# A two-block kernel on one core: reordered entries into three stages, work moved to GpSimd, and the residual ahead of the modulation's products

## The reference, cut to what matters

```python
h_lat = h_lat + m_lat[2] * o_lat                      # layer 0: RWKV and Mamba mixer
h_lat = h_lat + m_lat[5] * _swiglu(_modulate(_rms_norm(h_lat, g), m_lat[3], m_lat[4]), w1, w3, w2)
# and the same for h_ctx
def prepare(h):                                       # in the mixer
    z = h @ w_in
    z_rw = _centred_shift(z[..., :RW_COLS], rw_mu[0], rw_mu[1])
    ...
    bonus_f = jnp.sum(rh * k_dir[:, :, 0] * rw_r_k[0], axis=-1, keepdims=True)
    bonus_b = jnp.sum(rh * k_dir[:, :, 1] * rw_r_k[1], axis=-1, keepdims=True)
    bonus = (bonus_f + bonus_b) * vh
    xbc = jax.nn.silu(_centred_dwconv(xbc, mb_conv_w, mb_conv_b))
    dt = jax.nn.softplus(dt_raw + mb_dt_bias)
    a_neg = -jnp.exp(mb_a_log)
m_lat = jnp.split(c_lat_act @ w_ada[i] + b_ada[i], 6) # the modulation, of every layer
out = sum(gates[..., e] * _swiglu(h, w1[e], w3[e], w2[e]) for e in range(8))  # layer 1: top 2 of 8 experts
```

## Time and profile before

| | us |
|---|---|
| runs | 3094.3, 3093.96, 3085.2 |
| median | 3093.96 |
| profiled execution, its own time | 3092.86 |
| its span, first to last instruction | 3091.1 |
| PE busy | 2966.1 |
| DVE busy | 1315.6 |
| ACT busy | 539.9 |
| mean granted TensorE clock | 0.980 of full speed |

### The profile page before, as it was taken

How to read it: one execution, slowest core, us unless ns; L and a number is a source line. 1 busy time by engine, 2 the same in 40 slices (tenths; PEclk the granted TensorE clock), 3 DMA queues, 4 the chain that set the end, 5 groups by cost and what they waited for, 6 DMA issues and landing times.

```text
span 3091.1 us, 50586 instructions
## 1 busy us (share of the span) xinstructions
PE 2966.1 (96%) x21484; PEld 1949.7 (63%) x21484; DVE 1315.6 (43%) x3023; ACT 539.9 (17%) x1200; POOL 0.2 (0%) x4
## 2 busy tenths in 40 slices
PE   7999899999999998999999999999999899999998
PEld 5455699994444443557745555445558678877887
DVE  1467788875998977403321111111111432023211
ACT  2113433321211111203310000000011310022000
POOL 0000000000000000000000000000000000000000
PEclk9999899999999999999989999999999999999999
DMA  7232001004776885320189999999972235522451
GB/s 267 94 136 81 1 1 42 1 15 136 231 238 226 250 239 164 136 95 15 51 329 378 373 370 375 378 392 387 373 272 91 79 105 154 145 87 68 150 150 55
DMA packets 351331, 551.01 MB, mean 178 GB/s; under 512 B 14256, under 2 KB 292144, under 8 KB 347792
## 3 DMA queue, kind: packets, MB, share of 16 engines
q1 hardware_dynamic: 351120, 547.89, 50.3%
HBM read 546.80 MB, written 1.05 MB: 177 GB/s over the span
## 4 chain that ended last, share of the span: by engine, by line
PE 90%; DVE 5%; ACT 2%; DMA 2%; issue 1%; SPq 0%; DVEq 0%; ACTq 0%
PE bank L675 16%; PE bank L1342 15%; PE bank L1134 9%; PE bank L1358 7%; PE bank L1535 7%; PE bank L936 7%; PE bank L1148 4%; PE bank L634 3%; PE bank L754 3%; PE bank L1175 2%; PE bank L1079 2%; DVE mix L2093 2%; PE bank L920 1%; DMA arena<-in_ada_w 1%; PE bank L1209 1%; PE bank L1301 1%
## 5 line engine op out<-in xcount | busy, mean ns | idle before, releaser
L675 PE MATMUL bank<-a,ring 128*128 128x256 f32 (+1 forms) x1792 | 451.2, 414 | 8.9 <-DVE a L2028 6.6
L2093 DVE SCALAR_TENSOR_TENSOR mix<-arena,csil,mix 128x256 f32<-128x256 f32 x1008 | 402.1, 477 | 45.9 <-ACT mix L1638 45.9
L675 PEld LDWEIGHTS bank<-a,ring 128*128 128x128 f32 x1792 | 340.6, 191 | 116.2 <-issue 64.2
L1342 PE MATMUL bank<-ring,arena 128*32 128x352 f32 x5376 | 404.8, 461 | 4.8 <-DVE small L2652 4.8
L1342 PEld LDWEIGHTS bank<-ring,arena 128*32 128x32 f32 x5376 | 176.8, 110 | 227.8 <-issue 226.8
L1134 PE MATMUL bank<-a,ring 128*128 128x512 f32 x704 | 307.6, 597 | 6.8 <-ACT a L1634 6.8
L1134 PEld LDWEIGHTS bank<-a,ring 128*128 128x128 f32 x704 | 133.2, 191 | 179.9 <-issue 177.9
L1535 PE MATMUL bank<-arena,ring 128*128 128x256 f32 x1024 | 223.5, 379 | 2.0 <-DVE arena L2805 2.0
L2688 DVE TENSOR_TENSOR arena<-arena,bank 128x352 f32<-128x352 f32 x48 | 25.0, 521 | 443.4 <-ACT arena L1902 443.4
L1358 PE MATMUL bank<-ring,arena 128*32 128x256 f32 x3840 | 213.3, 379 | 0.0
L1535 PEld LDWEIGHTS bank<-arena,ring 128*128 128x128 f32 x1024 | 194.4, 190 | 29.1 <-DVE arena L2805 2.8
(11 more groups left out here) (416 smaller groups left out, 3195.7 us busy)
## 6 DMA issues: line engine op xcount, KB each, us to landing
ring<-in_moe_w SPq DMA_DIRECT2D x224, 704.0 KB, 9.2
ring<-in_moe_w SPq DMA_DIRECT2D x160, 512.0 KB, 6.7
ring<-in_mlp_w SPq DMA_DIRECT2D x64, 1024.0 KB, 5.4
arena<-in_ada_w SPq DMA_DIRECT2D x96, 512.0 KB, 3.8
arena<-in_w_ada SPq DMA_DIRECT2D x48, 512.0 KB, 3.5
ring<-in_ffn_w SPq DMA_DIRECT2D x22, 1024.0 KB, 8.3
arena<-in_moe_w SPq DMA_DIRECT2D x32, 704.0 KB, 10.0
h<-in_w_ada SPq DMA_DIRECT2D x8, 2048.0 KB, 7.4
```

Source lines behind the costliest of these rows:

```text
L675: i = mm(bank[b][:, 0:n], ws[:, k, t * P:t * P + P], rhs[:, k, sl], start=(k == 0), stop=(k == KT - 1))
L1342: i = mm(b[32 * t:32 * t + 32, 0:PART], ac_[:, g, 32 * k:32 * k + 32], by_tile(ws[i_], t), start=(k == 0), stop=(k == KT - 1), skip_group_ ...
L2093: ins = V.scalar_tensor_tensor(dst, x, cond, dst, ALU.mult, ALU.add)
```

## The change

Six edits; the computation stays as it is.

1. Mamba's entry. PE does half of `rkv_tile(0)`, turns chunks 0 and 1 as soon as the SiLU tiles that each needs are there, then `gram`, a quarter of `rkv_tile(0)`, chunks 2 and 3, the last quarter, `cs`, `decay(0)` and `rkv_tile(1)` without the wait for `shift(0)`. ACT does the softplus after the second `xbc` copy, DVE's part comes ahead of convolution 5.
2. `keys_by_query` of j = 0 and 1, as four operations each, and the clearing of `state` go to GpSimd.
3. In the second product the residual and its square stand ahead of the modulation's products and first parts of that step.
4. At the experts' entry the turning of the gathered tokens and the two marks come ahead of the overflow order.
5. The output leaves in four DMAs of 256 KB.

The sixth is only the place of `cs` and `shift(0)` on DVE, behind `xdt`. The diff, cut:

```diff
@@ sync
-            sy.wait_ge(act_done, at(AC, ("norm", 12, KT - 1, 1)))
-            sy.dma_start(out.rearrange("(k p) n -> p k n", p=P), hT[:, :, LAT]).then_inc(stored, 16)
-            sy.wait_ge(stored, 16)
+            for k in range(0, KT, 2):
+                sy.wait_ge(act_done, at(AC, ("norm", 12, k + 1, 1)))
+                sy.dma_start(out.rearrange("(k p) n -> p k n", p=P)[:, k:k + 2, :], hT[:, k:k + 2, LAT]
+                             ).then_inc(stored, 16)
+            sy.wait_ge(stored, 4 * 16)
@@ tensor
-            rkv_tile(0)
+            rkv_tile(0, range(0, 4))
+            pe.wait_ge(act_done, at(AC, ("zg", 3)))
+            pe.wait_ge(act_done, at(AC, ("xb", 3)))
+            turned_x(0)
+            turned_x(1)
+            pe.wait_ge(act_done, at(AC, ("xb", 5)))
+            turned_b(0)
+            turned_b(1)
             pe.wait_ge(act_done, at(AC, ("xb", 7)))
...
             i.then_inc(pe_done, did(PE, "gram"))
+            rkv_tile(0, range(4, 6))
+            pe.wait_ge(vec_done, at(VE, ("bt", 0)))
+            turned_x(2)
+            turned_b(2)
+            pe.wait_ge(vec_done, at(VE, ("bt", 1)))
+            turned_x(3)
+            turned_b(3)
+            rkv_tile(0, range(6, KT))
...
+                    if u == 0:
+                        rkv_tile(1)
                     pe.wait_ge(vec_done, at(VE, ("shift", u)))
-                    rkv_tile(u + 1)
+                    if u:
+                        rkv_tile(u + 1)
...
-                pe.wait_ge(vec_done, at(VE, ("rk", j)))
+                if j < 2:
+                    pe.wait_ge(pool_done, at(GP, ("rk", j)))
+                else:
+                    pe.wait_ge(vec_done, at(VE, ("rk", j)))
@@ scalar
+            for j in range(2):
+                xbc_copy(j)
             ac.wait_ge(vec_done, at(VE, "dt_raw"))
...
             act(a_neg, row("mb_a_log", 16), ACT.Exp).then_inc(act_done, did(AC, "a_neg"))
+            for j in range(2, 8):
+                xbc_copy(j)
+            for j in range(8):
+                ac.wait_ge(vec_done, at(VE, ("conv", j)))
+                act(xb[:, j, :], xb[:, j, :], ACT.Silu).then_inc(act_done, did(AC, ("xb", j)))
...
             for k in range(KT):
-                if k + 1 < KT:
-                    first_parts(pairs_of(FT + k + 2))
                 later_rows_out(FT + k)
                 ac.wait_ge(vec_done, at(VE, ("ffn res", k)))
                 square(2, slice(0, T), k)
+                if k + 1 < KT:
+                    first_parts(pairs_of(FT + k + 2))
...
+            counts.count[ACM] = per
+            act(small[:, 700:701], ident[:, 0:1], ACT.Copy).then_inc(ac_moe, per)
             ac.wait_ge(vec_done, at(VE, "blocks"))
-            counts.count[ACM] = per
-            act(small[:, 700:701], small[:, 604:605], ACT.Copy).then_inc(ac_moe, per)
@@ gpsimd (new)
+            for j, spare in ((0, 1), (1, 3)):
+                gp.wait_ge(vec_done, at(VE, ("kd", 1, j)))
+                G.tensor_scalar(kdka[:, j, :], kd[0][:, j, :], col("rw_r_k", j), None, ALU.mult
+                                ).then_inc(pool_done, did(GP, ("rk 0", j)))
+                G.tensor_scalar(kdka[:, spare, :], kd[1][:, j, :], col("rw_r_k", 4 + j), None, ALU.mult
+                                ).then_inc(pool_done, did(GP, ("rk 1", j)))
+                gp.wait_ge(pool_done, at(GP, ("rk 1", j)))
+                G.tensor_tensor(kdka[:, j, :], kdka[:, j, :], kdka[:, spare, :], ALU.add
+                                ).then_inc(pool_done, did(GP, ("rk 2", j)))
+                gp.wait_ge(pool_done, at(GP, ("rk 2", j)))
+                G.tensor_tensor(kdka[:, j, :], kdka[:, j, :], r_[:, j, :], ALU.mult
+                                ).then_inc(pool_done, did(GP, ("rk", j)))
+            gp.wait_ge(pe_done, at(PE, ("rk", 3)))
+            G.memset(state, 0.0).then_inc(pool_done, did(GP, "state 0"))
@@ vector
             for j in range(8):
+                if j == 5:
+                    ve.wait_ge(act_done, at(AC, "a_neg"))
+                    op("dtv", ...)
+                    op("a_tok", ...)
                 ve.wait_ge(act_done, at(AC, ("xbc", j)))
...
+            turned_out(0)
+            turned_out(1)
             ve.wait_ge(more_in, 16)
             ve.wait_ge(pe_done, at(PE, "gram"))
...
-            shift(0)
+            turned_out(2)
+            turned_out(3)
...
+                if d == 0:
+                    ve.wait_ge(pe_done, at(PE, "cs"))
+                    V.tensor_copy(small[:, 192:256], bank[6][:, 0:64]).then_inc(vec_done, did(VE, "cs"))
+                    shift(0)
...
-            for j in range(4):
-                keys_by_query(j)
+            keys_by_query(2)
+            ve.wait_ge(pool_done, at(GP, ("rk 2", 1)))
+            keys_by_query(3)
...
-            op("state 0", V.memset(state, 0.0))
...
+                    if u == 0:
+                        ve.wait_ge(pool_done, at(GP, "state 0"))
...
             for n in range(KT):
+                ve.wait_ge(pe_done, at(PE, ("ffn out", n)))
+                residual("ffn res", n, bank[2 + n % 4], (0, 0, 5), (0, 1))
                 if n + 1 < KT:
                     products_by_partition(pairs_of(FT + n + 2))
-                ve.wait_ge(pe_done, at(PE, ("ffn out", n)))
-                residual("ffn res", n, bank[2 + n % 4], (0, 0, 5), (0, 1))
                 columns_out(FT + n - 1)
...
+            ve.wait_ge(pe_done, at(PE, "gather first"))
+            for g in range(GROUPS_OF):
+                gathered(g, vec_done, VE, "gathered first")
+            ve.wait_ge(vec_done, now(VE))
+            counts.count[VEM] = per
+            V.memset(small[:, 701:702], 0.0).then_inc(ve_moe, per)
             for i in range(2):
                 op(("order part", i), ...)
```

More of the change, by code:

```diff
@@ L747, in turned, with rkv_tile, turned_x, turned_b @@
                 i.then_inc(pe_done, did(PE, name))
-            def rkv_tile(n):
+            def rkv_tile(n, ks=range(KT)):
                 s, m = first["rkv"] + n // 2, 96 if RKV[n] == 13 else P
                 ws = full(s)
-                for k in range(KT):
+                for k in ks:
                     i = mm(bank[RKV_BANK[n]][0:m, :], ws[:, k, n % 2 * P:n % 2 * P + m], aT[:, k, :],
                            start=(k == 0), stop=(k == KT - 1), skip_group_check=True)
-                i.then_inc(pe_done, did(PE, ("rkv", n), *([("slot", s)] if n % 2 else [])))
-            rkv_tile(0)
-            pe.wait_ge(act_done, at(AC, ("xb", 7)))
-            pe.wait_ge(act_done, at(AC, ("zg", 3)))
-            for c in range(NCH):
-                cs_ = slice(c * P, c * P + P)
-                if c >= 2:
-                    pe.wait_ge(vec_done, at(VE, ("bt", c - 2)))
-                turned(("xt", c), lambda m: xb[:, m, cs_], 2 + c % 2)
-                turned(("bt", c), lambda m: xb[:, 4 + m, cs_], 4 + c % 2, 2)
+                if k == KT - 1:
+                    i.then_inc(pe_done, did(PE, ("rkv", n), *([("slot", s)] if n % 2 else [])))
+            def turned_x(c):
+                turned(("xt", c), lambda m: xb[:, m, c * P:c * P + P], 2 + c % 2)
+            def turned_b(c):
+                turned(("bt", c), lambda m: xb[:, 4 + m, c * P:c * P + P], 4 + c % 2, 2)
+            rkv_tile(0, range(0, 4))
[6 more added lines that the diff above has]
+            turned_b(1)
+            pe.wait_ge(act_done, at(AC, ("xb", 7)))
             for g in range(2):
@@ L1655, in _, with xbc_copy @@
             ac.wait_ge(vec_done, at(VE, "xpad edges"))
-            for j in range(8):
+            def xbc_copy(j):
                 ac.wait_ge(pe_done, at(PE, ("xbc", j)))
@@ L1659, in _ @@
                      bank[j % 2].rearrange("p (s t) -> p s t", s=2))
-            for j in range(8):
-                ac.wait_ge(vec_done, at(VE, ("conv", j)))
-                act(xb[:, j, :], xb[:, j, :], ACT.Silu).then_inc(act_done, did(AC, ("xb", j)))
+            for j in range(2):
+                xbc_copy(j)
             ac.wait_ge(vec_done, at(VE, "dt_raw"))
@@ L1992, in _ @@
             norm(12, LAT)
+        @block.gpsimd
+        def _(gp):
+            G = nc.gpsimd
+            for j, spare in ((0, 1), (1, 3)):
[12 more added lines that the diff above has]
+            G.memset(state, 0.0).then_inc(pool_done, did(GP, "state 0"))
         @block.vector
@@ L2155, in _, with turned_out @@
                                                     ALU.mult, ALU.add))
[L2156 to L2162 removed]
+            def turned_out(c):
                 ve.wait_ge(pe_done, at(PE, ("xt", c)))
@@ L2639, in _ @@
             op("blocks", V.tensor_copy(block_info[0:1, 0:14], info[0:1, 0:14]))
-            per = at(VEM, ("per", "moe"))
-            pper, aper = at(PEM, ("per", "moe")), at(ACM, ("per", "moe"))
-            def gathered(g, inc, counter, name):
-                V.transpose(ac_[:, g, :], bank[4 * (g // 2)][:, 256 * (g % 2):256 * (g % 2) + 256]
-                            ).then_inc(inc, did(counter, (name, g)))
```

(6 more changed lines are left out.)

22 lines of the change are left out of this document (12 added, 10 removed).

## The result

The kernel after takes 3063.11 us (median of 4 runs, 3059.61 to 3065.98), the kernel before 3091.78 us beside it (4 runs, 3085.2 to 3094.3): a ratio of 0.991, 95% interval 0.9893 to 0.9927. 3066 was predicted, within 3057 to 3077. The profiled execution after took 3064.43 us, 28.4 less than that of before, and its span is 28.5 us shorter. One execution of the kernel before that ran beside e9 to e12 took 11892 us in the chip's slow state and is left out of every figure here.

The account below looks back on a forecast made before the run. TensorE was taken as the bound, busy 2966 of 3091 us; gains of 8.6 (Mamba's entry), 1.4 (keys), 12.0 (residual), 3.2 (experts' entry) and 1.6 (end) sum to 26.8, from 3092.86 to 3066.1 us, range 3057 to 3077.

Parts of the forecast that it names:

- Rival B: Mamba's entry: the clock stays low there, so the gain is 3 us, total 3071.7 us; chance 0.12.
- Rival C: RWKV units: the earlier start from Mamba's entry is given back there, total 3074.7 us; chance 0.07.
- PE then becomes the bound: Ahead of the RWKV units: PE's rk sums, not DVE, set the start of `decays(0)`, limiting the gain to 1.4 us.
- Rival A: Keys ahead of the RWKV units: DVE and GpSimd hold each other up, 3.7 us lost, total 3069.8 us; chance 0.12.
- rival D: Second product: late loads for the modulation's products starve the sums, 33 us lost, total 3111 us; chance 0.03.

Follow-up runs that it names:

- e9: Kernel after, with GpSimd doing only the single-tensor operation of all four key groups and VectorE the two-tensor ones; 3064.04 us, ratio 0.9915.
- e12: Kernel after with dt spread among zg, single-tensor keys on GpSimd, output in eight pieces, unread products in three idle stretches; 3055.32 us, ratio 0.9889.
- e5: Kernel before, waits kept, with unread products keeping TensorE busy in four idle stretches; 3089.73 us, ratio 0.999.
- e2: Kernel before with the new order of Mamba's entry alone; 3085.71 us, ratio 0.998.
- e3: Kernel before with the new order of the experts' entry alone; 3085.05 us, ratio 0.9978.
- e10: Kernel before with only the dt products spread among the second half of zg; 3089.15 us, ratio 0.9993.

## Why the prediction was right, point by point

**Mamba's entry: right.** 8.6 us predicted, 8.56 measured. The waits are 0.85 and 0.38 us (0.65, 0.1 and 0.65 in the sum), the clock 1.00, and e5 confirms the split that the sum used: 4.0 us of the gain are clock. Rival B (clock low there) had its mark, a clock of 0.5 between transposes and `rkv_tile(1)`, and it came in none of the nine traces with the edit. Rival C (given back in the units) fell too: in e2, with this part alone, the way from `rkv_tile(1)` to `decays(0)` is as long as before within 0.01 us.

**Keys on GpSimd: right in sign, half in size.** 1.4 us predicted, 0.7 measured. The step that failed is "PE then becomes the bound": in the trace after PE's sums end 20.0 us behind the first w0 sum, and DVE's last `bonus`, for which `decays(0)` waits, at 21.1. The holds cost DVE 3.3 us. Rival A gave DVE 1.9 us in hand, counted to its first `bonus`; by the same rows it had 2.7, as its four `bonus` operations take 2.48 us and PE's sums 3.5. So 0.6 to 0.7 us of the gain were lost. Rival A's mechanism is shown, at a smaller size: three holds of 1.07 us for the four of 1.4 that it priced, and 0.7 us lost of the expected gain and not 3.7. The Trainium skill (SBUF — State Buffer, SBUF: two separate sides) calls the port pair of the two engines "an exclusive lock, not a bandwidth split"; the DVE rows that end 0.54 us behind a GpSimd operation of two tensors agree. That it is held for the whole instruction, which the prediction took from there, does not fit e9, where a DVE operation ran in 0.68 us within one GpSimd operation and the next ended 0.34 us ahead of its end. The Trainium skill's GPSIMD Engine Reference (Performance versus the Vector engine) has a two-input operation at about twice VectorE's time; 1.27 to 1.60 us against 0.69, 1.8 to 2.3 times, agrees.

**Residual first: right.** 12.0 predicted, 12.33 measured, 9.3 of it waits and 2.8 the clock that the earlier trace rows showed behind the long one. The nearness owes something to the one trace that both were read from: the low clock behind that wait cost 1.5 to 1.6 us in e2, e3 and e10. No sum waited for a modulation's product, so rival D had nothing to start from: DVE's step has the 3 us in hand that the prediction gave it.

**Experts' entry: right in mechanism, too small.** 3.2 predicted, 5.9 measured, over the upper bound of 3.3. The wait gave 3.08. The mis-sized term is the other 2.8 us, the low clock behind the wait. The prediction priced this effect at Mamba's entry and in the second product and left it out here, since it read only PE's waits at this place and no window behind them; the window of 1563 to 1567 us was there to be read.

**The end: right.** 1.6 predicted, 2.0 measured, just over the bound of 1.9; 256 KB landed in 2.2 us and not the 2.8 on the line of the earlier trace rows, one of whose two points was a load. The figures that the prediction quotes from the Trainium skill (DMA: Bandwidth & Descriptors, Anatomy of one DMA) stand there for DMAs that GpSimd issues, and these stores are issued by SP; by them a piece of 256 KB would take 2.6 us, an estimate, where 2.2 was measured.

**The sum.** The parts came to 29.5 us and not 26.8. The profiled time fell by 28.4, as stages that the change doesn't touch lost 1.1 us in balance, with single ones between +3.3 and -3.5. So the closeness of 3066 and 3063 is partly luck: a part missed by 2.7 us, and noise of its own size.

## What to carry to other kernels

Behind the long waits of TensorE (2.7 to 7.9 us here) read the granted clock as well, and in more than one trace: the low stretches cost 1.5 to 4.6 us a stage, as much as a short wait, and they went when the wait went or when the wait was filled. A block of very narrow products is such a place too, with no idle time in it; spread among wide ones it kept the clock up in four traces of four, and gained 5 us on one of the two kernels that it was tried on alone. Before work goes to GpSimd to relieve VectorE, look at what VectorE does meanwhile: with two inputs in SBUF on VectorE, more than half of the relief was paid back in holds.

## What the runs showed of the hardware

- The granted clock fell to 0.50 within 64 gapless instructions of 128x16, in ten traces of ten (and within 32 of 128x8 in e12, with filled time ahead of them), and stayed at 1.00 in four of four where the same products stood 16 instructions at a time among products of 256 columns.
- VectorE operations with two SBUF inputs that began during a GpSimd operation of two tensors ended 0.54 to 0.55 us behind it, in all four cases of the trace after, three of them 1.07 us longer than usual; beside GpSimd operations of one tensor the hold was 0.41 us four times in e9, with the held operation over 0.34 us ahead of GpSimd's, and none in the trace after, where an operation of 0.68 us began at 312.85, 0.28 us ahead of the end of one. A GpSimd operation of 128x512 took 1.27 to 1.60 us with two tensors and 1.56 to 2.46 us with one: the simpler was not the quicker.
- A stage with no wait over 1 us and at the higher clock throughout, as Mamba's entry and the second product are after the edits, repeats within 0.05 us from trace to trace. The same stages with their long waits moved by 1.5 to 1.6 us over four traces, and other untouched stretches by up to 4 us. So a stage tells what an edit is worth sooner than the time does, if the stage before is read in several traces.
